# Turning attention weights with a diagonal of factors, in place of scaling them first and turning them with the identity

## The reference, cut to what matters

```python
s_c = einsum(q, k_cmp) * scale + bias;  p_c = masked_softmax(s_c);  o_c = p_c @ v_cmp   # 31 compressed keys
s_s = einsum(q, k_sel) * scale + bias;  p_s = masked_softmax(s_s);  o_s = p_s @ v_sel   # selected keys
s_w = einsum(q, k_w)   * scale + bias;  p_w = masked_softmax(s_w);  o_w = p_w @ v_w     # window keys
return g[..., 0:1] * o_c + g[..., 1:2] * o_s + g[..., 2:3] * o_w
```

## Time and profile before

| | us |
|---|---|
| median of 3 runs | 1873.64 (1873.5 to 1875.53) |
| the profiled execution | 1875.62 |
| its span, first to last instruction | 1873.9 |
| attention loop, first turn to last product's start | 418.5 to 581.1 |
| TensorE busy in the span | 1684.0 (90%) |
| VectorE busy | 751.7 (40%) |
| ScalarE busy | 435.1 (23%) |

### The profile page before, as it was taken

The page is one execution under the profiler, slowest core; times in us unless marked ns, Lnnn a source line. Parts: engine busy times, 40 slices in busy tenths (PEclk is TensorE's granted clock), DMA queues, the critical chain, the costliest instruction groups (busy, mean ns, idle before and its releaser), DMA issues. The chain is left out here.

```text
span 1873.9 us, 21968 instructions
## 1 busy us (share of the span) xinstructions
PE 1684.0 (90%) x8078; PEld 955.9 (51%) x8078; DVE 751.7 (40%) x1907; ACT 435.1 (23%) x1081; POOL 112.4 (6%) x130
## 2 busy tenths in 40 slices
PE   6999999899998999999987777778899999998777
PEld 2656555476667888756322222222368555633222
DVE  5445445765556654463111111010555554321114
ACT  3323223214452000023111010101222431222211
POOL 1100000100000000000000000000100000011100
PEclk9999999999999999999999999999999999899999
DMA  8742335951120622476999999999712234699996
GB/s 346 265 157 101 121 136 200 405 195 43 43 76 24 268 91 90 174 323 231 420 428 427 427 427 427 426 427 426 277 45 75 91 139 202 235 419 426 426 425 246
DMA packets 67879, 474.61 MB, mean 253 GB/s; under 512 B 11381, under 2 KB 12597, under 8 KB 45632
## 3 DMA queue, kind: packets, MB, share of 16 engines
q1 hardware_dynamic: 51168, 398.76, 52.7%
q0 software_dynamic: 15456, 70.32, 9.6%
q10 hardware_dynamic: 1152, 4.19, 0.5%
HBM read 458.58 MB, written 34.64 MB: 263 GB/s over the span
## 5 line engine op out<-in xcount | busy, mean ns | idle before, releaser
L2243 PE MATMUL moe_ps<-moe_up,moe_hg 128*64 128x512 f32 x1536 | 354.4, 608 | 96.2 <-DMA moe_up<-in_exp_up 36.7
L2243 PEld LDWEIGHTS moe_ps<-moe_up,moe_hg 128*64 128x64 f32 x1536 | 111.2, 139 | 333.8 <-issue 231.1
L2275 PE MATMUL moe_ps<-moe_down,moe_midT 128*64 128x512 f32 x720 | 163.8, 598 | 21.5 <-DMA moe_down<-in_exp_down 19.2
L534 PE MATMUL mx_pair<-hT,hg_w 128*128 128x512 f32 x336 | 149.1, 596 | 1.7 <-DMA hg_w<-in_w_hg 1.7
L2351 ACT ACTIVATE moe_sig<-moe_ps 128x512 f32<-128x512 f32 (+1 forms) x32 | 15.7, 491 | 521.6 <-PE moe_ps L2243 521.6
L2380 DVE COPY moe_midT<-moe_ps 128x512 f32<-128x512 f32 (+1 forms) x32 | 17.9, 558 | 258.8 <-PE moe_ps L2256 258.8
L2390 DVE SCALAR_TENSOR_TENSOR moe_res<-moe_ps,moe_route_slot_share,moe_gain 128x512 f32<-128x512 f32 x64 | 45.1, 746 | 178.5 <-PE moe_ps L2275 178.5
L2275 PEld LDWEIGHTS moe_ps<-moe_down,moe_midT 128*64 128x64 f32 x720 | 49.4, 136 | 115.0 <-issue 86.6
L534 PEld LDWEIGHTS mx_pair<-hT,hg_w 128*128 128x128 f32 x336 | 62.1, 190 | 74.2 <-issue 73.4
L2372 DVE TENSOR_TENSOR moe_mid<-moe_sig,moe_ps 128x512 f32<-128x512 f32 (+1 forms) x32 | 17.7, 554 | 136.8 <-PE moe_ps L2243 134.3
L557 PEld LDWEIGHTS mx_pair<-hg_w,hT 128*128 128x128 f32 x512 | 58.3, 192 | 4.1 <-issue 3.3
(11 more groups left out here) (476 smaller groups left out, 2628.1 us busy)
## 6 DMA issues: line engine op xcount, KB each, us to landing
moe_down<-in_exp_down SPq DMA_DIRECT2D x44, 2048.0 KB, 37.3
moe_up<-in_exp_up SPq DMA_DIRECT2D x31, 2048.0 KB, 37.8
moe_up<-in_exp_gate SPq DMA_DIRECT2D x31, 2048.0 KB, 37.9
moe_up<-in_exp_in SPq DMA_DIRECT2D x31, 2048.0 KB, 32.9
rest_w<-in_mod_rest POOLq DMA_DIRECT2D x16, 1536.0 KB, 9.6
hg_w<-in_w_hg SPq DMA_DIRECT2D x32, 512.0 KB, 3.8
rest_w<-in_mod_rest POOLq DMA_DIRECT2D x8, 2048.0 KB, 8.6
xn<-in_w_merge SPq DMA_DIRECT2D x32, 512.0 KB, 4.3
```

Of the source, the lines that this page charges most:

```text
L534: last = pe.matmul(proj[bank][:, :], w[s][:, kc, :], k.hT[:, kc, :], start=(kc == 0), stop=(kc == KC - 1))
L2243: last = pe.matmul(self.up_ps[u][e * SLOTS:(e + 1) * SLOTS, :], self.hg[m % 2][:, kc, e * SLOTS:(e + 1) * SLOTS], w[:, e, kc % 4, :], star ...
L2275: last = pe.matmul(self.res_ps[side][e * SLOTS:(e + 1) * SLOTS, :], self.midT[:, f, e * SLOTS:(e + 1) * SLOTS], w[:, e, side * 512:(side + ...
```

## The change

The unit's weights stay unnormalized in `p[u]`. VectorE no longer scales them; it builds a 128x128 diagonal from the identity, with `factor` times the gate of each query on it, in one of four buffers. TensorE multiplies each block of `p[u]` with that diagonal by an ordinary matmul, which turns and scales at once. Before it writes a diagonal, VectorE waits until the turn that used the buffer last is done. The compressed unit stays as it was.

```diff
@@ sparse_attention
         spare = k.sb(ctx, "at_spare", [P, 2])
+        diag = [k.sb(ctx, f"at_diag{n}", [P, P]) for n in range(4)]
@@ def turn(h, u)
                         for kk in range(UNITS[u][1] + 1):
-                            last = pe.transpose(tr[u % 2][:, kk * P:(kk + 1) * P], p[u][:, kk * P:(kk + 1) * P], k.const("ident"))
+                            last = pe.matmul(tr[u % 2][:, kk * P:(kk + 1) * P], p[u][:, kk * P:(kk + 1) * P], diag[u % 4][:], start=True, stop=True, skip_group_check=True)
@@ def normalized(h, u)
                     if u < len(UNITS):
                         br, c = UNITS[u]
-                        n = (c + 1) * P
-                        dve.tensor_scalar(buf[:, 0:n], buf[:, 0:n], factor[:, u, 0:1], gates[:, c, bass.ds(h * 3 + (1 + br), 1)],
+                        if u >= 4:
+                            dve.wait_ge(S["turned"], h * NU + (u - 3))
+                        elif after_first(h):
+                            dve.wait_ge(S["turned"], (h - 1) * NU + (u + 5))
+                        dve.tensor_scalar(diag[u % 4][:], k.const("ident"), factor[:, u, 0:1], gates[:, c, bass.ds(h * 3 + (1 + br), 1)],
                                           ALU.mult, ALU.mult).then_inc(S["p_ready"], 1)
```

## The result

The changed kernel takes 1882.4 us (median of 11 runs, 1879.94 to 1885.99) against 1875.53 (11 runs, 1872.8 to 1879.41). The ratio over all runs is 1.0041, with a 95% interval of 1.0033 to 1.0048: **7.7 us slower, 6.2 to 9.0** (the two medians by themselves are 6.9 apart). Forecast was 9.6 us slower. The same kernel again (experiment 8) gave 1.0048, 1.0035 to 1.0060.

What follows compares the result with a forecast made beforehand. TensorE was taken to bound seven heads and VectorE the last; +10.1 us in the seven and -0.5 in the last gave +9.6, so 1873.64 us becomes 1883.2. The 8-in-10 range was 1879.5 to 1891.5.

Steps and rivals of the forecast that it cites:

- A product is two records at 0.111 us, a turn one: TensorE's turns of units 0 to 7: 160 added records, 17.8 us over 8 heads before any hiding.
- rival 4: TensorE's turns: a product costs four turns, about +41 us, 1915; chance 0.02.
- The longer weight load: TensorE's loads, 191 ns against 141: costed at nothing beside the matmuls, upper bound 16 us.
- Units 6 and 7 are hidden behind a chain of 4.83 us: End of each of seven heads, compressed unit's scores to its turn: 0.78 us added fits into 1.0 of waits.
- units 0 to 5 are paid: Seven heads: 13 blocks a head paid in full, 1.44 us a head, +10.1 us.
- VectorE's cut of 6.4 us: Narrower VectorE writes, 0.8 us less a head; comes through only in the last head, which VectorE holds.
- eight new waits: Last head, VectorE: each new semaphore wait costs some 0.04 us, taken off the cut of 0.8.
- The new wait never holds: VectorE ahead of each diagonal: the wait finds its count reached, costing only its issue, 0.03 to 0.06 us a unit.
- The delay goes to the end one to one: Merge and everything after the attention: starts 9.6 us later and keeps its length.
- The last head's: Last head: TensorE's added 2.2 us fit into lost time, VectorE's cut comes through: -0.5 us, bounds -0.8 to +2.2.

Runs made afterwards that it cites:

- experiment 8: The changed kernel again, unaltered, for more runs and a second profile; ratio 1.0048 to the kernel before.
- experiment 1: Kernel before, with the turns of units 0 to 7 as ordinary products with the identity and VectorE scaling as before; stage +10.15 us, ratio 1.0047.
- experiment 7: Kernel before, with the shortened chain at each head's end and diagonals in the last head alone; stage -5.26 us, ratio 0.9965, 1868.41 us.
- experiment 2: Kernel before, with the change on units 6 and 7 only; stage -0.33 us, ratio 1.0001.
- experiment 3: Kernel before, with the change on units 0 to 5 only; stage +9.68 us, ratio 1.0053.
- experiment 6: Kernel before, with the compressed unit scaled in one instruction and its mask put into the gate ahead of the loop; stage -4.44 us, ratio 0.9975, 1871.26 us.
- experiment 4: Changed kernel with turns back to transposes, diagonals built but unread, factor and gate left out; stage -0.81 us, whole time 3933.84 us.
- experiment 5: Changed kernel with eight diagonals in place of four and without the added wait; seven heads 155.46 us, last head 16.50, ratio 1.0040.

## Why the prediction was right, by its steps

- **A product is two records at 0.111 us, a turn one.** Right: 320 records, +10.15 us from the product alone (experiment 1), against 10.1 worked out. The factor is two, and not the four of rival 4. The longer weight load (192 ns) cost nothing, as costed. The general rule of the Trainium skill, "Perfetto Trace Analysis", section Transposes (use the transpose, not a plain matmul), holds in the seven heads that TensorE bounds. Where TensorE idles, in the last head, it costs nothing to break it (experiments 1 and 7).
- **Units 6 and 7 are hidden behind a chain of 4.83 us, units 0 to 5 are paid.** Right, and shown from both sides by experiments 2 and 3. The room in this stretch was read 0.1 us too small: in the kernel before, TensorE also loses time ahead of `mix` of unit 6 (0.55 us from 431.69 to 432.24 for two records that take 0.43 in the changed kernel), and so 0.34 us stayed free, and not 0.2. Experiment 6 shows what the hiding place is: shorten the chain and the time falls by the wait that was in it.
- **VectorE's cut of 6.4 us is worth only the last head's 0.8.** Right in kind (experiment 4: -0.81). I took 0.04 us off for each of eight new waits and so had -0.5; that term was too large. Experiment 5 prices the waits at nothing in the stage, and the trace shows that no register operation came with them. In the last head, which is written out, the gap ahead of a diagonal is the same 0.08 us with the wait and without.
- **The new wait never holds.** Right (experiment 5). The releaser named in the profile would have misled.
- **The delay goes to the end one to one.** Right: from the merge's start to the end it is 1290.5 us before and 1290.5 after in the first pair of profiles; all the others but that of experiment 4 lie at 1288.4 to 1291.8, both kernels among them, without an order. The stretches in which the page of the kernel before has 426 to 428 GB/s took back nothing.
- **The size of the whole.** 9.6 forecast; 9.4 in the stage; 7.7 (6.2 to 9.0) and 9.0 (6.6 to 11.3) by the two comparisons of runs. The stage's sum was right to 0.2 us; for the whole program 9.6 lies outside the first interval and inside the second. Two terms were off. The last head's was, by 0.3 us. And one was missing: I took the stages ahead of the change as equal, where the seven profiles of the two kernels have them 2.5 us shorter. With it the spans should differ by 6.9, and they do by 7.5 (means 1873.5 and 1881.0). Why they are shorter is not known.

## What to carry to other kernels

Here work was moved from VectorE, busy for 83 of 145 us in seven heads, to TensorE, busy for 140 of them (97%). It was paid in full, except for what lay inside a stretch that a chain of other engines holds anyway. To find out how much that is in another kernel, take the chain's start and end in the timeline and count the added instructions between them. The same look shows where the gain is: here the chain itself, four small scalings and a mask at each head's end, was worth 4.4 us, where 6.4 us cut from the same engine elsewhere were worth 0.8.

## What the runs showed of the hardware that was not expected

- Ahead of all that was changed, the first transfers landed earlier in the changed kernel, and its first turn came 2.5 us earlier in the mean of four profiles against three. So a difference of this size (0.13%) between two programs can arise at a place that their code shares; what causes it, and how much of it the unprofiled runs have, is open.
- A new semaphore wait, placed in the loop beside an operation with a register operation of its own, left the register operations at 32. It added 0.7 us to VectorE's idle time in 32 places and nothing measurable to the seven heads: 155.4 to 155.5 us with it, 155.46 without.
- Records behind a wait took longer than in a stream. Eight records of a turn behind VectorE's weights took 0.99 us to the next work in experiment 1 (430.46 to 431.45), and six of `mix` behind ScalarE's copy 0.77 in experiment 6; in the changed kernel's stream eight took 0.89:

```profile
422.96 1.06 PE L1169 MATMUL at_tr<-at_diag,rest_w 128*128 128x128 f32 x8
423.85 0.81 PE L1154 MATMUL mx_pair<-at_kvT,at_q 128*128 128x384 f32 x2
```
